# Decode tile in fp32 column groups, units fetched ahead of the conditioning pairs, one low part ahead of the fold: a two-layer retention and sparse-attention step on one core

## What is computed

```python
def block(x, c, l, mixer, ...):
    mod = (jax.nn.silu(c) @ w_mod[l] + b_mod[l])[:, None, :]      # the conditioning
    sh1, sc1, g1, sh2, sc2, g2 = jnp.split(mod, 6, axis=-1)
    y, st = mixer(x * (1 + sc1) + sh1)
    x = layer_norm(ALPHA * x + g1 * y, ln1_g[l], ln1_b[l])
    f = grouped_moe(x * (1 + sc2) + sh2, ...)                     # 16 experts, top 2 of one group
    return layer_norm(ALPHA * x + g2 * f, ln2_g[l], ln2_b[l]), st

def retention_mixer(h, s0, w_in, gn_g, w_out, cos, sin):          # layer 0: 4 heads, dk 256, dv 512
    q, k, v, g = jnp.split(h @ w_in, [...], axis=-1)
    q, k = rotate(q, cos, sin), rotate(k, cos, sin) * RET_DK ** -0.5
    o, s = retention_scan(q, k, v, s0)                            # chunks of 128; decode rows: one step from s0
    return (group_norm(o) * silu(g)) @ w_out, s
```

## Time and profile before

| | us |
|---|---|
| runs, median of 3 (lowest to highest) | 2042.51 (2042.26 to 2043.4) |
| the profiled execution, its own time | 2042.13 |
| span in the profile (first to last instruction) | 2040.4 |
| TensorE (PE) matmul busy | 1714.7 (84%) |
| VectorE (DVE) busy | 1244.5 (61%) |
| ScalarE (ACT) busy | 871.3 (43%) |
| GpSimd (POOL) busy | 101.7 (5%) |
| mean TensorE clock granted, share of full | 0.892 |
| chain that ended last: PE, DMA, DVE, ACT | 63%, 13%, 10%, 5% |

### The profile page before, as it was taken

The page is one execution under the profiler, slowest core; times in us unless marked ns, Lnnn a source line. Parts: engine busy times, 40 slices in busy tenths (PEclk is TensorE's granted clock), DMA queues, the critical chain, the costliest instruction groups (busy, mean ns, idle before and its releaser), DMA issues.

```text
span 2040.4 us, 22705 instructions
## 1 busy us (share of the span) xinstructions
PE 1714.7 (84%) x7697; PEld 1194.7 (59%) x7697; DVE 1244.5 (61%) x1824; ACT 871.3 (43%) x1028; POOL 101.7 (5%) x149
## 2 busy tenths in 40 slices
PE   3779999999999984999997479997887929999980
PEld 0556546774577632878774266554636627878760
DVE  1432364433644356988984833588525768988867
ACT  1222233332341043878773322332532227878751
POOL 0000010000000002000001100001000020000001
PEclk8789999999999976999998569997867959999995
DMA  9556763216523369999998511115000439999963
GB/s 338 185 189 236 266 243 114 93 62 209 204 92 127 126 248 333 367 391 394 391 392 314 178 54 54 62 32 171 6 22 29 164 132 375 390 391 394 391 248 125
DMA packets 200177, 435.29 MB, mean 213 GB/s; under 512 B 15961, under 2 KB 20073, under 8 KB 199054
## 3 DMA queue, kind: packets, MB, share of 16 engines
q1 hardware_dynamic: 174338, 339.04, 46.4%
q0 software_dynamic: 18384, 73.10, 9.4%
q10 hardware_dynamic: 7374, 22.12, 3.2%
HBM read 379.96 MB, written 66.85 MB: 219 GB/s over the span
## 4 chain that ended last, share of the span: by engine, by line
PE 63%; DMA 13%; DVE 10%; ACT 5%; issue 4%; DVEq 3%; ACTq 1%; POOL 1%; SPq 0%; POOLq 0%
PE bank L688 28%; PE bank L1080 17%; PE bank L672 4%; DMA RING<-in_w_gate 3%; DMA RING<-in_w_up 3%; ACT WH L1606 2%; DMA RING<-in_w_in_ret 2%; PE bank L710 2%; PE bank L981 1%; DVE WL L2425 1%; PE bank L1005 1%; DMA RING<-in_w_in_dsa 1%; PE bank L679 1%; DMA RING<-in_w_mod 1%; PE bank L1206 1%
## 5 line engine op out<-in xcount | busy, mean ns | idle before, releaser
L2425 DVE TENSOR_TENSOR WL<-RING,WH 128x2048 fp32r<-128x2048 f32 x192 | 435.8, 2288 | 63.9 <-ACT WH L1606 63.1
L688 PE MATMUL bank<-RINGR,HTH 128*128 128x512 f32 (+3 forms) x1440 | 463.5, 405 | 0.8 <-DVE HTL L1988 0.5
L1606 ACT ACTIVATE WH<-RING 128x2048 fp32r<-128x2048 f32 x192 | 364.9, 1916 | 119.0 <-PE bank L1080 102.7
L688 PEld LDWEIGHTS bank<-RINGR,HTH 128*128 128x128 f32 (+1 forms) x1440 | 246.8, 179 | 106.2 <-issue 27.5
L688 PE MATMUL bank<-RINGR,HTL 128*128 128x512 f32 (+3 forms) x720 | 286.5, 399 | 0.0
L672 PE MATMUL bank<-cst,M 128*128 128x128 f32 (+3 forms) x721 | 117.3, 295 | 155.4 <-DMA M<-h_d 55.6
L1979 DVE TENSOR_TENSOR RINGR<-RING,RINGR 128x2048 fp32r<-128x2048 f32 (+1 forms) x48 | 105.7, 2214 | 181.1 <-ACT RINGR L1375 180.8
L1080 PE MATMUL bank<-WH,HGH 128*128 128x512 f32 x512 | 204.9, 400 | 3.4 <-DVE HGL L2434 3.4
L672 PEld LDWEIGHTS bank<-cst,M 128*128 128x128 f32 (+3 forms) x721 | 94.4, 158 | 190.2 <-DMA M<-h_d 56.6
L1080 PE MATMUL bank<-WH,HGL 128*128 128x512 f32 x512 | 201.8, 394 | 0.0
L1080 PE MATMUL bank<-WL,HGH 128*128 128x512 f32 x512 | 201.8, 394 | 0.0
(11 more groups left out here) (306 smaller groups left out, 2216.7 us busy)
## 6 DMA issues: line engine op xcount, KB each, us to landing
RING<-in_w_gate SPq DMA_DIRECT2D x64, 1024.0 KB, 10.7
RING<-in_w_up SPq DMA_DIRECT2D x64, 1024.0 KB, 11.2
RING<-in_w_down SPq DMA_DIRECT2D x64, 1024.0 KB, 11.3
RING<-in_w_mod SPq DMA_DIRECT2D x48, 1024.0 KB, 8.7
RING<-in_w_in_ret SPq DMA_DIRECT2D x24, 1024.0 KB, 5.6
RING<-in_state_ret SPq DMA_DIRECT2D x16, 1024.0 KB, 6.9
out_ret_sample<-RING POOLq DMA_DIRECT2D x16, 1024.0 KB, 5.9
h_d<-y_d POOLq DMA_DIRECT2D x8, 1536.0 KB, 7.2
```

The lines of the kernel that those rows point to most:

```text
L688: last = pe.matmul(out, x_[:, c, :], w_[:, c, :], start=start and c == n == 0, stop=stop and c == 3 and n == 2)
L1606: act.activation(WH[:, u % SPLIT, :, :], raw(u % RAW), ACT.Copy).then_inc(S("hi_rdy"), 1)
L2425: TT(WL[:, u % SPLIT, :, :], raw(u % RAW), WH[:, u % SPLIT, :, :].bitcast(F32), ALU.subtract)\
```

## The change

The change has six parts.

1. In 34 units, the decode tile's 12 fp32r matmuls are replaced by four fp32 matmuls from the raw weights, in four column groups (`few_unit`), like a conditioning pair. The units are those of retention blocks 1, 2, 3, 5, 6, 7, 8, 9 and 11, all of `out0` and `out2`, and two blocks of `din`. Since `low` writes over the raw weights, these matmuls stand in the unit before: in its second tile (t == 1) in the retention blocks and its first in the out products and `din`. VectorE's `low` of such a unit waits for them (`few_ps`). After the last unit of a block ScalarE copies the bank (`take_few`) and one matmul adds the groups up (`few_sum`).
2. In `seg0.keys` each q, k, v unit that stood behind a conditioning pair is fetched ahead of it.
3. In the state stage the broadcasts of v read an fp32r operand `VHL` with the high and the low part stacked in 40 rows, where before they read v in fp32 with 8 rows. It is made by VectorE (clear), ScalarE (copy of the high part) and VectorE (difference), a chain on the semaphore `v_step`.
4. The transposes of q, k and y use one bank (2) where they took turns between two; the copy `MP` of a conditioning pair has one buffer where it had two; banks of the out products are numbered anew.
5. In `mixer_close`, for m = 0 the low parts of the second half are placed as (1, 0), the first half's sums, (1, 1), (1, 2), fold, (1, 3); for m = 2 as (1, 0), the first half's sums, (1, 1), fold.
6. In `din` the low part of a unit's second half stands behind the block's rotations for the two blocks concerned.

The core of the diff:

```diff
         assert late == len(LATE)
+        at = 2 * EARLY + 1
+        while at + 3 < len(seg0.keys):
+            kinds = [key[0] for key in seg0.keys[at:at + 3]]
+            if kinds[:2] == ["mod", "mod"] and kinds[2] in "qkv":
+                seg0.keys[at:at + 3] = seg0.keys[at + 2:at + 3] + seg0.keys[at:at + 2]
+                at += 1
+            at += 1
         for n in range(2):
...
         D_BANK = (0, 1, 4, 5, 6)
-        O_BANK = (D_BANK, (2, 3, 7, 0, 1))
+        O_BANK = (D_BANK, (2, 7, 0, 1, 4))
+        O_FEW = (7, 3)
+        FEW_BLOCKS = [blk for blk in range(len(BLOCKS)) if blk and blk % 6 != 4]
+        FEW = [BLOCKS[blk] + (h,) for blk in FEW_BLOCKS for h in range(2)] + [("out0", n, kq) for n in range(2) for kq in range(4)] \
+            + [("din", D_ORDER[i], h) for i in (1, 2) for h in range(2)] + [("out2", n, kq) for n in range(2) for kq in range(2)]
+        FEW_AT = {key: i for i, key in enumerate(FEW)}
+        FEW_LAST = [i for i, key in enumerate(FEW) if key[-1] == (3 if key[0] == "out0" else 1)]
         tiles_of = [(TILES + 1) // 2, TILES // 2]
...
                 return last
+            taken = 0
+            def few_unit(key):
+                wait_slot(pe, key)
+                bk, x_, first, final = bank[3], DX, key[-1] == 0, FEW_AT[key] in FEW_LAST
+                if key[0] == "out0":
+                    bk, x_ = bank[O_FEW[key[1]]], DXY
+                    pe.wait_ge(S("yt_ev"), (key[2] + 1) * TILES)
+                elif key[0] == "out2":
+                    bk = bank[O_FEW[key[1]]]
+                    pe.wait_ge(S("op_hi"), 5)
+                elif key[0] == "din":
+                    bk = bank[7]
+                if first:
+                    pe.wait_ge(S("few_ev"), sum(i < FEW_AT[key] for i in FEW_LAST))
+                w = slot(key)
+                for c in range(4):
+                    last = pe.matmul(bk[32 * c:32 * c + DEC, :], x_[:, 4 * key[-1] + c, :], w[:, c, :], start=first, stop=final)
+                last.then_inc(S("few_ps"), 1)
+            def few_sum(out, part):
+                nonlocal taken
+                taken += 1
+                pe.wait_ge(S("few_ev"), taken)
+                return pe.matmul(out[0:DEC, :], C("sel")[:, 0:DEC], part[:, :], start=True, stop=True)
             def wait_split(key):
...
                         for t in range(TILES):
-                            if kq == 0 and n == 1 and t >= 3:
-                                pe.wait_ge(S("out_ev"), TILES * m + t - 2)
-                            last = unit_mm(bank[O_BANK[n][t]][0:rows(t), :], xh[:, :, cols(t)], xl[:, :, cols(t)],
-                                           (f"out{m}", n, kq), kq == 0, kq == quarters - 1)
+                            if n == 1 and (kq == 0 and t in (2, 3) or kq == quarters - 1 and t == NT):
+                                pe.wait_ge(S("out_ev"), TILES * m + t - 1)
+                            if t < NT:
+                                last = unit_mm(bank[O_BANK[n][t]][0:rows(t), :], xh[:, :, cols(t)], xl[:, :, cols(t)],
+                                               (f"out{m}", n, kq), kq == 0, kq == quarters - 1)
+                            elif kq == quarters - 1:
+                                last = few_sum(bank[O_BANK[n][t]], FEW_OUT[m])
                             if n == kq == 0:
...
                                 last.then_inc(S("out_mm"), 1)
-                            elif t == NT:
+                            elif t == NT - 1:
                                 last.then_inc(S("out_half"), 1)
+                            if t == 0:
+                                following = (f"out{m}", n, kq + 1) if kq < quarters - 1 else (f"out{m}", 1, 0)
+                                if (n, kq) != (1, quarters - 1):
+                                    few_unit(following)
             pe.nop().then_inc(S("unit_used"), UNIT0)
...
                 wait_split(key + (h,))
+                few = key + (h,) in FEW_AT
                 for t in range(TILES):
                     before(h, t)
-                    if h == 0 and blk:
+                    if (h == 1 if few and t == NT else h == 0) and blk:
                         pe.wait_ge(S("ret_ev"), (blk - 1) * TILES + t + 1)
-                    last = unit_mm(bank[D_BANK[t]][0:rows(t), :], *h_tile(t, h), key + (h,), h == 0, h == 1)
+                    if t < NT or not few:
+                        last = unit_mm(bank[D_BANK[t]][0:rows(t), :], *h_tile(t, h), key + (h,), h == 0, h == 1)
+                    elif h:
+                        last = few_sum(bank[D_BANK[t]], FEW_RET)
                     if h == 1:
                         last.then_inc(S("ret_mm"), 1)
-                    elif t == NT:
+                    elif t == (NT - 1 if few else NT):
                         last.then_inc(S("ret_half"), 1)
+                    if t == 1:
+                        following = key + (1,) if h == 0 else unit_after(blk)
+                        if following in FEW_AT:
+                            few_unit(following)
                     if t == (1 if h else 3):
...
                     if b == 0:
-                        pe.wait_ge(S("qk_rd"), hp + 1)
+                        pe.wait_ge(S("q_step"), 2 * hp + 2)
+                        pe.wait_ge(S("v_step"), 3 * hp + 3)
                     for hh in range(2):
...
                             pe.wait_ge(S("st_upd"), si - 1)
-                        pe.matmul(bank[1 + hh][:, :], ident[0:DEC, b:b + 1].to_broadcast([DEC, P]),
-                                  V[0:DEC, NT, hh * NB:(hh + 1) * NB], start=True, stop=True).then_inc(S("vb_ps"), 1)
+                        pe.matmul(bank[1 + hh][:, :], pick[:, b:b + 1].to_broadcast([32 + DEC, P]),
+                                  VHL[:, hh * NB:(hh + 1) * NB], start=True, stop=True).then_inc(S("vb_ps"), 1)
                 query_keys()
...
                 act.wait_ge(S("mod_pp"), 2 * i + 2)
-                if i >= 2:
+                if EARLY <= i < NEXT_AT:
+                    act.wait_ge(S("mod_mm"), i)
+                elif i >= 2:
                     act.wait_ge(S("mod_mm"), i - 1)
                 act.activation(part[:, :], src[:, :], ACT.Copy).then_inc(S("mod_pv"), 1)
+            taken = 0
+            def take_few(bk, part):
+                nonlocal taken
+                taken += 1
+                act.wait_ge(S("few_ps"), FEW_LAST[taken - 1] + 1)
+                act.activation(part[:, :], bk[:, :], ACT.Copy).then_inc(S("few_ev"), 1)
             mod_at = EARLY
...
                 split(*BLOCKS[blk], 1)
+                if blk in FEW_BLOCKS:
+                    take_few(bank[3], FEW_RET)
             def next_block(blk):
...
                         take_qk()
+                act.wait_ge(S("v_step"), 3 * hp + 1)
+                act.wait_ge(S("ret_ev"), (6 * hp + 4) * TILES)
+                act.activation(VHL[0:DEC, :], V[0:DEC, NT, :], ACT.Copy).then_inc(S("v_step"), 1)
                 for i in range(2 * NT):
...
                 dve.wait_ge(S("w_hi"), place[key][5] + 1)
+                if key in FEW_AT:
+                    dve.wait_ge(S("few_ps"), FEW_AT[key] + 1)
                 w = unit_width(key)
...
                 T = EPT[m]
-                if m == 2:
-                    low("out2", 1, 0)
-                    low("out2", 1, 1)
+                low(f"out{m}", 1, 0)
                 dve.wait_ge(S("ep_in"), 64 * m + 64)
...
                     moments(m, t, n)
-                if m == 0:
-                    low("out0", 1, 0)
-                    low("out0", 1, 1)
                 for t in range(TILES):
                     add_half(0, t)
+                low(f"out{m}", 1, 1)
                 if m == 0:
                     low("out0", 1, 2)
-                    low("out0", 1, 3)
-                else:
+                if m == 2:
                     dve.wait_ge(S("kv_st"), 16 * 3 * TILES)
                 fold(m, HN[1])
+                if m == 0:
+                    low("out0", 1, 3)
                 for s in range(TILES + 2):
...
                 dve.drain()
-                dve.engine_nop().then_inc(S("qm_rdy"), 1)
+                dve.engine_nop().then_inc(S("q_step"), 1)
                 for n in range(2):
...
                     next_block(6 * hp + 2 + n)
+                dve.wait_ge(S("ret_mm"), (6 * hp + 4) * TILES)
+                dve.memset(VHL[:, :].bitcast(F32), 0.0).then_inc(S("v_step"), 1)
+                dve.wait_ge(S("v_step"), 3 * hp + 2)
+                TT(VHL[32:32 + DEC, :], V[0:DEC, NT, :], VHL[0:DEC, :].bitcast(F32), ALU.subtract).then_inc(S("v_step"), 1)
                 def decay_att(i):
...
                     index_step(i, 0, t)
-                if i + 1 < 6:
+                few = i + 1 < 6 and ("din", D_ORDER[i + 1], 1) in FEW_AT
+                if i + 1 < 6 and not few:
                     low("din", D_ORDER[i + 1], 1)
...
                     index_step(i, 1, t)
+                if few:
+                    low("din", D_ORDER[i + 1], 1)
```

(6 more changed lines are left out.)

64 lines of the change are left out of this document (48 added, 16 removed).

## The result

The changed kernel takes **2003.91 us** (median of 5, 2001.37 to 2013.5) against 2042.51: a ratio of 0.9822 (95% interval 0.9806 to 0.9837), about 36 us less (33 to 40). Forecast were 62 us less, 1980, with a range of 1962 to 1999. The direction held, the size did not, and the time lies 5 us above the range.

A forecast was written before the change was run, and what follows sets the result against it. TensorE was taken to bound the first and later projections and state stage, waits the sparse projections, VectorE the second out product's end. Terms: 48.6 + 21 + 11.5 + 5 - 13.9 - 6 - 4 = 62.2; 2042.1 - 62.2 = 1980, range 1962 to 1999.

The forecast's parts named there:

- column groups, as priced: 34 decode units on TensorE at 0.95 us instead of 2.8, plus 15 sums of 0.95: 48.6 us saved.
- state broadcasts: State stage, 16 items: two broadcasts of v take 0.46 us instead of 1.91; about 21 us saved after added chain.
- fetch order: First q, k, v units fetched ahead: waits of 6.36 and 8.66 us and half clock go; 11.5 us saved net.
- sparse projections: Low part moved behind the rotations saves 1.8 us twice, a slow tile after a wait 1.5: 5 us saved.
- new waits: TensorE waits 1.5 to 1.8 us in blocks 5, 6, 7, 10 and 6.0 in the last g block; 13.9 lost overall.
- second out product: Its end is VectorE's, so TensorE's 5.5 us buys nothing and a moved low part costs 0.5: 6 us lost.
- clock after waits: Lower TensorE clock after five or six new waits: 4 us lost, between nothing and 11.
- rival C: Drain counted per tiling switch, 0.16 us exposed, two switches at 34 units: 11 us lost, 1991; chance 7%.
- Rival B: Units fetched ahead still land late because slots come free late: 11.5 us lost, 1992; chance 12%.
- D: State stage becomes bound by transfers, needing 351 GB/s: the 21 us is lost, 2001; chance 7%.
- E: Low part ends up in line before every tile needing it, 2.29 us at 34 units: slower, 2058; chance 3%.
- Rival A: New waits cost nothing, as VectorE finds gaps or y low parts are hidden: 13.9 + 4 return, 1962; chance 14%.

The follow-up runs named there:

- all_five: Changed kernel plus five edits: earlier decode matmuls, low part before rotation, y low parts first, ScalarE copy before split, second out product as before; 1972.77 us, ratio 0.967.
- din_take: Changed kernel with ScalarE's copy of the decode bank put ahead of the next unit's split in the sparse projections; 1992.33 us, ratio 0.9771.
- few_t0: Changed kernel with the early decode matmuls one tile sooner (first tile of the unit before) from block 4 on; 1996.6 us, ratio 0.9779.
- low_early: few_t0 with split and low part of the second half ahead of the fourth tile's rotation in blocks 7 and 8; 1989.5 us, ratio 0.976.
- only_order: Kernel before the change with the new fetch order alone; 2030.9 us, ratio 0.9954.
- only_state: Kernel before the change with the fp32r broadcasts of v in the state stage alone; 2026.78 us, ratio 0.9926.
- no_out2: Changed kernel with the second out product as before: 12 fp32r decode matmuls, both low parts ahead of the sums; 2003.32 us, ratio 0.9813.
- all_but_out2: all_five without its second out product edit, so column groups and the low part behind the sums stay there; 1974.01 us, ratio 0.9697.

## Why the forecast missed, step by step

| step | forecast | what the runs show |
|---|---|---|
| column groups, as priced | +48.6 | 34 x (2.79 - 0.97) - 15 x 0.96 = 47.5 by their own steps; by the length of the blocks and of the first out product 6.5 less (an estimate, below) |
| state broadcasts | +21 | 18.6 within the stages, 15 in the total |
| fetch order | +11.5 | 13.9 in its stage, 9 in the total |
| sparse projections | +5 | -3 and -6 in two profiles |
| new waits | -13.9 | 12.3 of those named, 4.2 and 4.3 not named |
| second out product | -6 | -6.6 to -7.3 |
| clock after waits | -4 | 3.3 in blocks 6 to 9, 1.6 and 2.9 in blocks 10 and 11 of two profiles, some 4 in the sparse projections |

(The sparse projections took 237.5 us before from first to last matmul, 235.2 and 238.3 after; the 5.5 that the first line counts there is taken off.)

**Right.** The waits of blocks 5, 6, 7, 10 and 11 came within 0.2 us of the working, with its reason (y at h + 15.3 against 9.3: 6.0, measured 5.98). The steps of a group of four and of a sum came within 3%.

**Right by the step, too high by the place: the price.** The prediction took the pair's step from the earlier trace rows and said that it held both switches. It doesn't: in the same rows the two matmuls behind the pair last 0.72, where two within a tile last 0.63 (437.20 above), and the neighbours of a group lose 0.2 us in all. Where TensorE doesn't wait and the clock is 1.00, the whole price can be read from the length of a block: block 8 takes 27.16 us in `all_five` instead of 29.29, and blocks 5, 6, 7, 8 and 11 are 2.07 to 2.16 shorter, not 2.75. In the changed kernel itself block 6 takes 29.15 with a wait of 1.63 in it, against 29.65 before. An estimate from these: 9 x 0.6 = 5.4 us less for the projection blocks. The first out product takes 99.5 us from first to last matmul's start instead of 112.5; of these 13.0, 1.2 go to its first group, which stands in block 11, so it gave 11.8 where 12.9 had been counted: 6.5 us less together.

The Trainium skill ("TensorEngine Tiling (Array Packing)", Key Properties) has TensorE drain at a change of the tiling mode. The 0.1 us on either side of a group would fit that, but the same steps stand around sums (0.32 ahead of the one at 416.99 in `all_five`, 0.34 behind it), and no run separates a drain from any other reason. Either way rival C, which counted 11 us for it, is right in part: some 6.5 by the estimate above.

**Wrong, first: the sparse projections.** The step "moved behind, 1.8 goes twice" looked at VectorE's queue and asked of ScalarE only when its eviction came. It did not ask what the change puts into ScalarE's own queue: the copy of the decode bank, behind a split that waits for a load, with TensorE waiting for the copy. Both gains that it named came: TensorE's wait for the first rotation is 7.75 us instead of 9.87, and the one of 2.03 is gone. But one of 4.7 to 4.8 took its place. That is the change's own wait for the sum's copy, of which the prediction told only the 0.9 us of its duration. `din_take` shows it.

**Wrong, second: blocks 6 to 9.** Each block was to be 2.75 shorter, less the waits before transposes. Without waits, in `all_five`, the four blocks take 109.40 us instead of 119.10. In the changed kernel, 1.63 + 1.62 for the named waits and 1.69 + 2.50 for the low parts bring that to 116.8, and 6.7 us at half clock behind the two waits for low parts (0.50 from 380.7 to 384.0, 0.53 from 414.6 to 418.0) cost the remaining 3.3: 120.1, measured 120.17. The step that failed is the sentence that only the rotations and y steps queued behind the low part are short of time. The low part behind the rotations was short too, since the tile that had covered it was what the change took away; this was cover to be named, at each block.

**Wrong, third: two waits for raw weights** (1.87 and 2.38) in the first projections. The early matmuls need a unit landed two tiles before the unit itself starts, in a stretch where DMA is 71% busy. "What hides it" was not asked for TensorE's new place. The terms gave 161.9 - 8.3 - 11.5 = 142.1 us for that stretch, measured 146.7, 15 us shorter than before and not the 20 to 25 named as the sign. These two waits are 4.3 us. They don't split the difference of 4.6 exactly: by the block lengths above three blocks bring some 1.8 less than 8.3, and the fetch order brought 13.9 by itself, not 11.5. The waits weren't tried by themselves, so that they cost their 4.3 us isn't shown: moved one tile later, the matmuls might only hand the delay on to the low part and the rotation (2.10 and 2.11 us late already).

**Too small: the clock.** -4 was set for all new waits; blocks 6 to 9 lost 3.3, blocks 10 and 11 2.9 and 1.6 in the two profiles (their length less that in `all_five`, less the waits of 1.53 and 5.98), and the sparse projections some 4 more. The half clock did not follow every wait: behind those of 1.5 to 1.6 the clock stayed at 1.00 (360.6 to 365.0, for one), behind that of 1.69 it was 0.50 in the changed kernel and 1.00 in `few_t0`. Once the waits were taken away, the clock's loss went with them (1.00 in blocks 6 to 9), which is why an edit could give more than the wait that it removed: 7.1 us of the stage for 4.2 in `low_early`.

**Close: broadcasts and second out product.** Two broadcasts step 0.66, not 0.46: 3.2 us over 16 items. The two step 0.34 and 0.32 where 0.23 was taken, like the neighbours of a group; why isn't settled. Of the low part that moved onto VectorE's path, 0.5 was taken as exposed where it is whole by its place; the stage lost 1.1 to 1.8.

Rival B (late units) falls with `only_order`, D (transfers) with `only_state`, E with the list of waits: there are seven new waits of over 1 us for a low part or for what stands behind it, not one at each of 34 units. Rival A, no cost of the waits, gave 1962; with most of the waits edited away the kernel takes 1973, and some 6.5 of these 11 us are the price of the groups as estimated above.

None of the signs that the prediction named for being wrong came: a group steps 0.97 us, a state stage lasts 53.6, the waits didn't grow in every block, and from the first expert matmul of the first layer to the sparse projections it takes 360.0 and 360.2 us against 360.9. They watched the prices and the rivals; the loss was in queues that none of them looked at.

## What to carry to other kernels

A cheaper operation takes its own cover away: list, for each queue of each engine, what the longer operation had been hiding, and cost that first. Where an operation is moved ahead of its old place, follow three lines: what it now waits for (a landing), what waits for it on the next engine, and what is queued behind that wait, a copy behind a split behind a load as much as a low part. Price an inserted instruction by the length of the whole block, for its neighbours can slow down beside it: here 0.2 us beside steps of 0.97. Some waits of 1.7 to 6 us on TensorE were followed by half clock, others of 1.5 to 2 weren't, so removing the last small waits of a stage could pay more than their sum.

## What the runs showed beyond that

Executions of one kernel differ by up to 15 us (2001.37 to 2013.5 for the changed kernel, 1995.8 to 2010.9 for `no_out2`, 1970.5 to 1985.9 for `all_but_out2`), and the kernel before by up to 11 (2034.9 to 2045.9 over the sessions), more than the 2 us of the first runs. Two profiles of the same kernel, 8 us apart, show most of their difference in a stretch where TensorE waits often: 93.80 us at a mean clock of 0.70 and 88.10 at 0.74. So about 0.2% was too fine a bound for what one set of runs can tell here; the intervals of the ratios above reach 0.14% to 0.26% to either side, and stage times told what totals could not.
